# Odd layer of a two-layer transformer kernel: conversions, head norms, projection blocks and the gate term rearranged

## The chip, the cores and the metric

The kernel runs on one core of a Trainium2 chip. The metric is the device time of one execution in microseconds (us); lower is better. The time before is the median of three runs.

## What is computed

The program runs a small transformer on 256 tokens of width 1024 in fp32: an even layer (convolution and gated linear attention), a sparse expert layer, an odd layer (attention with a forget gate), a second expert layer, and a second block with two further kinds of attention and a dense network. The change touches the odd layer alone:

```python
def fox_mix(h, w_in, fgate_b, q_g, k_g, w_out):
    q, k, v, fz = jnp.split(h @ w_in, [hd, 2 * hd, 3 * hd], axis=-1)   # 16 heads of 64
    q = rms_norm(q.reshape(B, S, 16, 64), q_g)
    k = rms_norm(k.reshape(B, S, 16, 64), k_g)
    c = jnp.cumsum(jax.nn.log_sigmoid(fz + fgate_b), axis=1)
    for each half of the 256 queries:
        logits = q @ k.T * scale + c[query] - c[key], masked causally
        o = softmax(logits) @ v[:hi]
    return o @ w_out
```

## The kernel before

Everything lies with its features on the 128 partitions. The input `h` of the odd layer is held as a rounded part `hhi` and a rest `hlo` in the type fp32r; a weight is split in the same way just before it is used. A **part** is 128 x 1024 weights. ScalarE copies it to `r_sh` (`hi`, L390), VectorE subtracts to get `r_sl` (`lo`, L396), and TensorE then makes three products for each 128 rows of the contraction. There are two buffers of each kind, so `hi` of part n waits until the products of part n-2 are done (L393).

`block_T` (L419, through `mm_T`, L402) makes 24 products of 256 columns for 128 outputs; it asks for `lo` only before its last eight. `parts_R` (L429) does a quarter of the product for v, 12 products of 512 columns, and asks for `lo` at its start. Each block ends in a PSUM bank, and ScalarE evicts it (`out_ac`, `v_ac`).

The odd layer (`odd`, L1480) has 25 parts of input weights: four for q of heads 0 to 7 (NQ), one narrow one for the gate (NF), four for k (NK), four for v (NV), and the same 4, 4 and 4 for heads 8 to 15 (NQ2, NK2, NV2). Eight parts of the output weights (OUT) follow. Before the change the work runs like this:

1. The 13 parts of the first half, in a row.
2. The head norm of q and that of k: ScalarE squares 128 x 1024 numbers (to `sq` or `sqk`), TensorE sums them per head (`head_norm_pe`, L522, two products of 512 columns in fp32, which the hardware runs as four instructions), ScalarE takes logarithm (two of 512 columns) and exponential, VectorE multiplies (`head_norm_ve`, L531). One part of NQ2 stands on TensorE behind each norm.
3. A loop over 16 heads (L1662), with two further steps for the pipeline to drain. TensorE makes the logits of head i (four fp32 products: query times key for the second and the first half of the queries, and for each the gate term, whose stationary operand is a column of the identity, repeated, and whose moving operand is `fz`, the cumulated gate), then up to two **fill** items, then the transposes of head i-2 (`soft_pe_b`, L1438), then the product with v of head i-3. VectorE adds the mask and takes the row maxima (`soft_ve_a`, L1459), ScalarE the exponentials with their sums (`soft_ac_a`, L1447), VectorE scales (`soft_ve_b`, L1468), ScalarE copies the transposed probabilities (`soft_ac_b`, L1453).
4. The fill items are the ten remaining parts and, last, the two head norms of heads 8 to 15 (`fill_pe`, L1641). They are used up by heads 0 to 5.
5. ScalarE splits the eight chunks of the attention output (`ohi`), VectorE their rests (`olo`), and after all of them TensorE makes the output projection (`mm_T` over OUT), with the sums of squares for the next norm between its blocks.

Each engine runs its own list in order. What sets it is the order in which these generators are advanced: `next(fill)` stands at the same place of the loop for every engine, and on ScalarE it stands between the exponentials of head i and the copy of head i-2:

```python
                if i < 16:
                    soft_ac_a(ac, "od", i, L, sm)
                next(fill, None)
                next(fill, None)
                if 2 <= i < 18:
                    soft_ac_b(ac, "od", i - 2, PT)
```

In `fill_ac` each item is `hi` of the next part, then the eviction of this one. Weights come by DMA into a ring of four slots, two megabytes at a time; SyncE issues a load when the last `lo` that reads the slot is done.

## Time and profile before

| | |
|---|---|
| median of three runs | 2628.95 us (2627.65 to 2629.12) |
| profiled execution | 2627.96 us, its span 2626.2 us |
| TensorE (PE) busy | 2501.7 us, 95% of the span |
| VectorE (DVE), ScalarE (ACT) busy | 1690.2 us (64%), 1299.1 us (49%) |
| chain that ended last | PE 90%, ACT 4%, DVE 4% |
| mean granted clock of TensorE | 0.971 of full speed |

The span is what the hardware profiler recorded between the first and the last instruction; the execution's own time is 1.8 us more. Busy times of different engines overlap. The chain is the sequence of instructions, each waiting for the one before, that ended last. The clock of TensorE has two levels, 1.2 and 2.4 GHz; a granted clock of 0.80 in a stretch means that part of it ran at the lower one. The odd layer takes some 200 of the 2626 us, from about 1069 to 1268 us.

### The profile page before, as it was taken

Reading aid. Unit: us, or ns where it says so; the run is one execution under the profiler, and the core shown is the slowest. Engines: PE = TensorE matmul, PEld = TensorE weight load, DVE = VectorE, ACT = ScalarE, POOL = GpSimd, SP = SyncE. Lnnn points to the kernel's source line nnn. Section 1 sums busy time; section 2 is a strip of 40 time slices with the busy share of each in tenths; the row PEclk is TensorE's granted clock in tenths of the full one; section 3 lists DMA queues with packets and bytes.
Section 4 is the critical chain, followed back from the end, with each engine's and each line's share of the span. In section 5 each row is a group of like instructions: output and inputs, shape, how many; then the busy total and the mean of one; then the engine's idle time right before and its main releaser. Section 6 shows DMA issues by size and latency. Waiting matters only on the chain.

```text
span 2626.2 us, 41667 instructions
## 1 busy us (share of the span) xinstructions
PE 2501.7 (95%) x16702; PEld 2281.8 (87%) x16702; DVE 1690.2 (64%) x3116; ACT 1299.1 (49%) x2451; POOL 432.2 (16%) x389
## 2 busy tenths in 40 slices
PE   7799999999999999888999999999999997997999
PEld 7689999999988888765999999998888886877999
DVE  4734899777777777434479977775555544534654
ACT  4234444666544444434444456665444543463543
POOL 4500000388400000000000018860000000001000
PEclk9799999999999999998999999999999997999999
DMA  6103455433487777520245543346555563213342
GB/s 252 45 33 129 157 184 182 161 129 129 160 279 259 257 267 264 220 75 22 97 161 184 181 166 129 130 138 210 194 195 193 197 227 123 97 65 128 140 182 81
DMA packets 93198, 421.81 MB, mean 161 GB/s; under 512 B 10296, under 2 KB 12880, under 8 KB 85072
## 3 DMA queue, kind: packets, MB, share of 16 engines
q1 hardware_dynamic: 93008, 419.16, 46.2%
q8 instruction: 134, 2.20, 0.3%
q14 instruction: 56, 0.46, 0.1%
HBM read 415.96 MB, written 3.16 MB: 160 GB/s over the span
## 4 chain that ended last, share of the span: by engine, by line
PE 90%; ACT 4%; DVE 4%; DMA 1%; issue 1%; POOL 0%; SPq 0%; POOLq 0%; ACTq 0%; DVEq 0%
PE PS L170 89%; ACT mem L181 2%; DVE mem L191 1%; ACT r_sh L181 1%; DVE hT L199 1%; DVE r_sl L191 1%; PE PS L173 0%; DMA mem<-in_ev_in 0%; ACT r_hhi L181 0%; POOL hT L191 0%; DVE mem L205 0%; DMA mem<-in_v 0%; DMA mem<-in_ada 0%; ACT L188 0%; DVE mem L202 0%
## 5 line engine op out<-in xcount | busy, mean ns | idle before, releaser
L191 DVE TENSOR_TENSOR r_sl<-mem,r_sh 128x1024 fp32r<-128x1024 f32 (+3 forms) x742 | 890.3, 1201 | 674.8 <-ACT r_sh L181 673.9
L181 ACT ACTIVATE r_sh<-mem 128x1024 fp32r<-128x1024 f32 (+3 forms) x742 | 764.9, 1033 | 482.0 <-PE PS L170 428.0
L170 PE MATMUL PS<-r_hhi,r_sh 128*128 128x256 f32 x3280 | 839.3, 292 | 37.5 <-ACT r_hhi L181 19.8
L170 PE MATMUL PS<-r_hlo,r_sh 128*128 128x256 f32 (+1 forms) x3152 | 795.8, 289 | 5.5 <-DVE r_hlo L191 2.6
L170 PEld LDWEIGHTS PS<-r_hhi,r_sh 128*128 128x128 f32 x3280 | 641.5, 196 | 46.5 <-issue 38.9
L170 PEld LDWEIGHTS PS<-r_hlo,r_sh 128*128 128x128 f32 (+1 forms) x3152 | 614.3, 195 | 14.5 <-DVE r_hlo L191 6.5
L170 PE MATMUL PS<-r_hhi,r_sl 128*128 128x256 f32 x3280 | 469.6, 286 | 0.3 <-DVE r_sl L191 0.3
L181 ACT ACTIVATE mem<-PS 128x256 f32<-128x256 f32 (+14 forms) x633 | 217.4, 353 | 475.1 <-PE PS L170 466.0
L170 PEld LDWEIGHTS PS<-r_hhi,r_sl 128*128 128x128 f32 x3280 | 431.6, 195 | 0.8 <-DVE r_sl L191 0.5
L196 POOL TENSOR_SCALAR xT<-cst,mem 128x128 f32<-128x128 f32 x256 | 327.6, 1291 | 620.8 <-ACT mem L181 557.0
L170 PE MATMUL PS<-r_sh,r_ch 128*128 128x512 f32 x1024 | 276.5, 391 | 1.3 <-ACT r_sh L181 1.3
L170 PE MATMUL PS<-r_sl,r_ch 128*128 128x512 f32 x1024 | 274.9, 389 | 0.0
L170 PE MATMUL PS<-r_sh,r_cl 128*128 128x512 f32 x1024 | 274.8, 389 | 0.0
L170 PEld LDWEIGHTS PS<-r_sh,r_ch 128*128 128x128 f32 x1024 | 191.0, 188 | 41.7 <-ACT r_sh L181 2.6
L170 PEld LDWEIGHTS PS<-r_sl,r_ch 128*128 128x128 f32 x1024 | 192.2, 188 | 40.2
L170 PEld LDWEIGHTS PS<-r_sh,r_cl 128*128 128x128 f32 x1024 | 192.2, 188 | 40.1
L170 PE MATMUL PS<-mem 64*128 64x128 f32 (+7 forms) x1010 | 177.4, 333 | 11.8 <-DVE mem L191 8.9
L170 PEld LDWEIGHTS PS<-mem 64*128 64x128 f32 (+4 forms) x1010 | 137.0, 177 | 48.6 <-issue 19.6
L170 PE MATMUL PS<-xT 128*128 128x128 f32 x1024 | 131.5, 277 | 4.0 <-DVE xT L191 4.0
L170 PEld LDWEIGHTS PS<-xT 128*128 128x128 f32 x1024 | 124.2, 194 | 4.3 <-issue 4.3
L191 POOL TENSOR_TENSOR hT<-xT,small 128x256 f32<-128x256 f32 x12 | 10.1, 841 | 713.7 <-ACT small L181 713.7
L191 DVE TENSOR_TENSOR r_cl<-mem,r_ch 128x256 fp32r<-128x256 f32 x256 | 107.1, 418 | 2.6 <-ACT r_ch L181 2.6
(129 smaller groups left out, 2137.3 us busy)
## 6 DMA issues: line engine op xcount, KB each, us to landing
mem<-in_u SPq DMA_DIRECT2D x256, 512.0 KB, 3.3
mem<-in_v SPq DMA_DIRECT2D x256, 512.0 KB, 3.9
mem<-in_w SPq DMA_DIRECT2D x16, 2048.0 KB, 8.0
mem<-in_ada SPq DMA_DIRECT2D x48, 512.0 KB, 4.5
mem<-in_in SPq DMA_DIRECT2D x9, 2048.0 KB, 7.9
mem<-in_wq SPq DMA_DIRECT2D x8, 2048.0 KB, 7.9
mem<-in_od_in SPq DMA_DIRECT2D x6, 2048.0 KB, 10.1
mem<-in_ev_in SPq DMA_DIRECT2D x5, 2048.0 KB, 10.6
```

What stands on the lines that cost most here:

```text
L170: return self.did(self.e and self.e.matmul(out, lhsT, rhs, start=start, stop=stop, skip_group_check=skip))
L181: return self.did(self.e and self.e.activation(out, in_, func, **kw))
L191: return self.did(self.e and self.e.tensor_tensor(out, a, b, op))
L196: return self.did(self.e and self.e.tensor_scalar(out, a, s1, s2, op0, op1))
L199: return self.did(self.e and self.e.scalar_tensor_tensor(out=out, in0=a, scalar=s, in1=b, op0=op0, op1=op1))
```

## The change

- **Conversions.** `hi` of a part in the head loop now stands behind the eviction of the part two before it, and the exponentials of a head no longer stand between the end of a block and the conversion that the very next block needs. `MORE` lists the 12 parts of the second half and, new, the first two of OUT.
- **Head norms.** Those of heads 0 to 7 are taken apart and put between the first 13 parts: the sum for q behind the seventh part on TensorE, that for k behind the second part of NV. Those of heads 8 to 15 stand in `BETWEEN` as `None`, behind part 5 and behind part 7.
- **Heads.** `BETWEEN` has 14 items, two for each of heads 0 to 6; the second one now stands behind the product with v, on all engines. All 12 parts of the second half are in it.
- **Gate term.** The cumulated gate is split in a rounded part (rows 0 to 15 of `cz`) and a rest (rows 32 to 47), with the first 128 columns repeated at 256 to 384. `two` has ones in rows h and 32+h of column h. One fp32r product of 384 columns replaces the two fp32 products of a head, and it stands first, ahead of the wait for the norm of k.
- **Output.** `ohi` and `olo` of a chunk are made during the heads (`SPLIT`), and the first block of the output projection waits for one chunk at a time.

The diff, cut to its core:

```diff
-    def mm_T(pe, n, out, s, start=True, stop=True, after_norm=None):
+    def mm_T(pe, n, out, s, start=True, stop=True, after_norm=None, after=None):
...
         for k in range(a):
             if after_norm is not None:
                 pe.wait_ge("hhi", after_norm, k)
+            elif after:
+                pe.wait_ge(after[0], k)
             pe.matmul(out, h[:, k, :], s[0][:, k, :], start and k == 0, False)
             if after_norm is not None:
                 pe.wait_ge("hloP" if k % 4 == 3 else "hlo", after_norm, k)
+            elif after:
+                pe.wait_ge(after[1], k)
             pe.matmul(out, h[:, k, :], s[1][:, k, :], False, False)
         pe.wait_ge("lo", n)
         for k in range(a):
...
+        cz = in_f32r("cz", o, 384)
+        take(384)
+        two = in_f32r("two", o, 16)
...
+        MAIN = NQ + NF + NK + NV
+        MORE = NQ2 + NK2 + NV2 + OUT[0:2]
+        BANK = (0, 1, 2, 3, 4, 5, 6, 7, 2)
+
+        BETWEEN = [0, 1, 2, 3, 4, 5, None, 6, 7, None, 8, 9, 10, 11]
+
+        SPLIT = {7: 0, 8: 1, 9: 2, 10: 3, 12: 4, 14: 5, 16: 6, 18: 7}
...
+        def between_ac(ac):
+            qs, ks = qf_[:, 1024:2048], kf_[:, 1024:2048]
+            norm = 0
+            for m in BETWEEN:
+                if m is None:
+                    src, rr = (("q", 1), r) if norm == 0 else (("k", 1), rk)
+                    ln_ac(ac, rr, (6, 7), src)
+                    exp_ac(ac, rr, src)
+                    norm += 1
+                else:
+                    n = MORE[m]
+                    if m < 8:
+                        out_ac(ac, (q if m < 4 else k_)[:, 4 + m % 4, :], n, 6 + m % 2)
+                    elif m == 11:
+                        v_ac(ac, n, (6, 7), 1)
+                    hi(ac, MORE[m + 2])
+                    if m == 4:
+                        square_ac(ac, qs, sq, NQ2[3], ("q", 1))
+                    elif m == 7:
+                        square_ac(ac, ks, sqk, NK2[3], ("k", 1))
                 yield
...
+            ns = MAIN + MORE
+            hi(ac, ns[1])
+            for i, n in enumerate(MAIN):
...
-            ac.wait_ge(*ac.activation(f1[0:16, :], z16, ACT.Abs).then_inc("actC"))
-            ac.wait_ge(*ac.activation(f1[0:16, :], f1[0:16, :], ACT.Exp, scale=-1.0).then_inc("actC"))
...
-            fill = fill_ac(ac)
-            norm_q_ac(ac, 0, (0, 1, 4, 5))
-            next(fill)
-            norm_k_ac(ac, 0, (0, 1, 4, 5))
-            next(fill)
+                    v_ac(ac, n, (3, 4), 0)
+                hi(ac, ns[i + 2])
+                if i == 4:
+                    square_ac(ac, qf_[:, 0:1024], sq, NQ[3], ("q", 0))
+                elif i == 5:
+                    ac.wait_ge("out", NF[0])
+                    ac.wait_ge(*ac.activation(f1[0:16, :], z16, ACT.Abs).then_inc("actC"))
+                    ac.wait_ge(*ac.activation(f1[0:16, :], f1[0:16, :], ACT.Exp, scale=-1.0).then_inc("actC"))
+                    ac.activation(f1[0:16, :], f1[0:16, :], ACT.Ln, bias=onet[0:16, :]).then_inc("softplus", 1)
+                elif i == 6:
+                    ln_ac(ac, r, (0, 1), ("q", 0))
+                elif i == 7:
+                    exp_ac(ac, r, ("q", 0))
+                elif i == 8:
+                    square_ac(ac, kf_[:, 0:1024], sqk, NK[3], ("k", 0))
+                elif i == 10:
+                    ln_ac(ac, rk, (0, 1), ("k", 0))
+                    exp_ac(ac, rk, ("k", 0))
+            between = between_ac(ac)
             for i in range(19):
                 if i < 16:
                     soft_ac_a(ac, "od", i, L, sm)
-                next(fill, None)
-                next(fill, None)
+                next(between, None)
                 if 2 <= i < 18:
                     soft_ac_b(ac, "od", i - 2, PT)
                 if i >= 3 and (i - 3) % 2:
                     h = i - 3
                     ac.wait_ge("pv", "od", h)
                     ac.activation(oT[:, h // 2, :], PS[:, 4 + (h // 2) % 2, 0:256], COPY).then_inc("oT", h // 2)
-            for c in range(8):
-                ac.wait_ge("oT", c)
-                ac.activation(hhiv[:, c, :], oT[:, c, :], COPY).then_inc("ohi", c)
+                next(between, None)
+                if i in SPLIT:
+                    c = SPLIT[i]
+                    ac.wait_ge("oT", c)
+                    ac.wait_ge("wdone", NV2[3])
+                    ac.activation(hhiv[:, c, :], oT[:, c, :], COPY).then_inc("ohi", c)
             for c, n in enumerate(OUT):
-                hi(ac, n)
                 if c >= 2:
+                    hi(ac, n)
                     square(ac, 3, c - 2)
...
+        def between_ve(ve):
+            for m in BETWEEN:
+                if m is not None:
+                    lo(ve, MORE[m + 2])
+                if m == 7:
+                    head_norm_ve(ve, qf_[:, 1024:2048], 1024, qg, r, ("q", 1))
+                elif m == 9:
+                    head_norm_ve(ve, kf_[:, 1024:2048], 1024, P("kg", 0), rk, ("k", 1))
                 yield
...
+            for i, n in enumerate(MAIN + MORE[0:2]):
+                if i:
+                    lo(ve, n)
+                if i == 7:
+                    ve.wait_ge("softplus", 1)
+                    ve.wait_ge(*ve.scalar_tensor_tensor(f2[0:16, :], z16, 0.0, f1[0:16, :], MIN, SUB).then_inc("dveC"))
+                    ve.wait_ge(*ve.tensor_scalar(f2[0:16, :], f2[0:16, :], -1.0, MUL).then_inc("dveC"))
...
+                    ve.wait_ge(*ve.tensor_copy(cz[0:16, 0:256], z16).then_inc("dveC"))
+                    ve.wait_ge(*ve.tensor_tensor(cz[32:48, 0:256], z16, cz[0:16, 0:256].bitcast(F32), SUB).then_inc("dveC"))
+                    ve.tensor_copy(cz[0:48, 256:384], cz[0:48, 0:128].bitcast(F32)).then_inc("forget", 0)
+                elif i == 9:
+                    ve.wait_ge("qg", 0)
+                    head_norm_ve(ve, qf_[:, 0:1024], 1024, qg, r, ("q", 0))
+                elif i == 12:
+                    head_norm_ve(ve, kf_[:, 0:1024], 1024, P("kg", 0), rk, ("k", 0))
+            between = between_ve(ve)
+            for i in range(20):
                 if 2 <= i < 18:
                     soft_ve_b(ve, "od", i - 2, L, sm)
                 if i < 16:
                     soft_ve_a(ve, "od", i, L, sm, C("fmask"))
-                next(fill, None)
-                next(fill, None)
+                next(between, None)
+                next(between, None)
+                if i - 1 in SPLIT:
+                    c = SPLIT[i - 1]
+                    ve.wait_ge("ohi", c)
+                    ve.tensor_tensor(olov[:, c, :], oT[:, c, :], hhiv[:, c, :].bitcast(F32), SUB).then_inc("olo", c)
...
-                lo(ve, OUT[c])
+                if c >= 2:
+                    lo(ve, OUT[c])
...
-        def fill_pe(pe):
-            ns = NQ2 + NK2
-            for i, n in enumerate(ns):
-                block_T(pe, n, 6 + i % 2, ("out", n))
+        def between_pe(pe):
+            turn = parts_R(pe, NV2, (6, 7), ("out", NV2[3]))
+            norm = 0
+            for m in BETWEEN:
+                if m is None:
+                    head_norm_pe(pe, 1024, (sq, sqk)[norm], (6, 7), ("qk"[norm], 1))
+                    norm += 1
+                elif m < 8:
+                    block_T(pe, MORE[m], 6 + m % 2, ("out", MORE[m]))
+                else:
+                    next(turn)
                 yield
-            yield from parts_R(pe, NV2, (6, 7), ("out", NV2[3]))
-            head_norm_pe(pe, 1024, sq, (6, 7), ("q", 1))
-            yield
-            head_norm_pe(pe, 1024, sqk, (6, 7), ("k", 1))
-            yield
...
-                block_T(pe, n, i % 7, ("out", n), after_norm=None if i else 2)
-            block_R(pe, NV, (2, 3), ("out", NV[3]))
-            fill = fill_pe(pe)
-            head_norm_pe(pe, 1024, sq, (0, 1), ("q", 0))
-            next(fill)
-            head_norm_pe(pe, 1024, sqk, (4, 5), ("k", 0))
-            next(fill)
+                block_T(pe, n, BANK[i], ("out", n), after_norm=None if i else 2)
+                if i == 6:
+                    head_norm_pe(pe, 1024, sq, (0, 1), ("q", 0))
+            for u, _ in enumerate(parts_R(pe, NV, (3, 4), ("out", NV[3]))):
+                if u == 1:
+                    head_norm_pe(pe, 1024, sqk, (0, 1), ("k", 0))
+            between = between_pe(pe)
             pe.wait_ge("forget", 0)
+            pe.wait_ge("two", 0)
             for i in range(19):
                 if i < 16:
                     h, b = i, i % 2
                     rows, c = slice(64 * (h % 2), 64 * (h % 2) + 64), h // 2
                     t1, t0 = PS[:, b, 0:256], PS[:, b, 256:384]
-                    pick = ident[:, h:h + 1].broadcast_to([128, 128])
                     bank_wait(pe, b)
+                    pe.matmul(PS[:, b, 0:384], two[:, h:h + 1].broadcast_to([128, 128]), cz[:, :], True, False, skip=True)
                     pe.wait_ge("hn", ("k", h // 8))
-                    pe.matmul(t1, q[rows, c, 128:256], k_[rows, c, :], True, False, skip=True)
-                    pe.matmul(t1, pick, fz, False, True, skip=True)
-                    pe.matmul(t0, q[rows, c, 0:128], k_[rows, c, 0:128], False, False, skip=True)
-                    pe.matmul(t0, pick, fz[:, 0:128], False, True, skip=True).then_inc("logits", "od", i)
+                    pe.matmul(t1, q[rows, c, 128:256], k_[rows, c, :], False, True, skip=True)
+                    pe.matmul(t0, q[rows, c, 0:128], k_[rows, c, 0:128], False, True, skip=True).then_inc("logits", "od", i)
                     emptied[b] = ("biased", "od", i)
-                next(fill, None)
-                next(fill, None)
+                next(between, None)
                 if 2 <= i < 18:
                     soft_pe_b(pe, "od", i - 2, L, None)
                 if i >= 3:
...
                     pe.matmul(out[:, 0:256], v[:, 0, 64 * h:64 * h + 64], PT[h % 2][:, 0:256], True, False, skip=True)
                     pe.matmul(out[:, 128:256], v[:, 1, 64 * h:64 * h + 64], PT[h % 2][:, 256:384], False, True, skip=True).then_inc("pv", "od", h)
                     emptied[b] = ("oT", h // 2)
-            for c in range(8):
-                pe.wait_ge("ohi", c)
-                pe.wait_ge("olo", c)
+                next(between, None)
             for c in range(8):
                 bank_wait(pe, c)
-                mm_T(pe, OUT[c], PS[:, c, 0:256], (hhiv, olov))
+                mm_T(pe, OUT[c], PS[:, c, 0:256], (hhiv, olov), after=None if c else ("ohi", "olo"))
                 emptied[c] = ("x", 2, c)
                 if c:
                     square_sum(pe, 3, c - 1)
```

The first head, on TensorE's list. `r_sl_54` and `r_sh_51` are split weights, `mem` the queries and keys (and `fz`), `cst` the identity, `r_cz` and `r_two` the two new tiles. Before:

```order
L170 MATMUL PS<-r_hhi,r_sl_54 128x256 x7
L170 MATMUL PS<-mem 128x256 [waits s_hn,s_hn_ln,s_forget]
L170 MATMUL PS<-mem,cst 128x256
L170 MATMUL PS<-mem 128x128
L170 MATMUL PS<-mem,cst 128x128
L170 MATMUL PS<-r_hhi,r_sh_51 128x256 [waits s_hi,s_out]
```

Now:

```order
L170 MATMUL PS<-r_sh_52,r_hlo 128x512 x2
L170 MATMUL PS<-r_cz,r_two 128x384 [waits s_hn_ln,s_two,s_forget]
L170 MATMUL PS<-mem 128x256 [waits s_hn]
L170 MATMUL PS<-mem 128x128
L170 MATMUL PS<-r_hhi,r_sh_51 128x256 [waits s_hi,s_out]
```

The head now comes straight behind the last part of NV (the row of 512 columns) instead of behind the second part of NQ2, and has one product of 384 columns and two others in place of four.

ScalarE's list from the exponentials of head 1. 128x1024 rows to `r_sh` are conversions, 128x256 rows from `PS` evictions, the 128x256 and 128x128 rows from `mem` the exponentials. Before:

```order
L181 ACTIVATE mem<-mem 128x256 [waits s_rowmax]
L181 ACTIVATE mem<-mem 128x128
L181 ACTIVATE r_sh_52<-mem 128x1024
L181 ACTIVATE mem<-PS 128x256 [waits s_wdone]
L181 ACTIVATE r_sh_51<-mem 128x1024
L181 ACTIVATE mem<-PS 128x256 [waits s_wdone]
```

Now, the same place:

```order
L181 ACTIVATE mem<-mem 128x256 [waits s_rowmax]
L181 ACTIVATE mem<-mem 128x128
L181 ACTIVATE mem<-PS 128x256 [waits s_wdone]
L181 ACTIVATE r_sh_51<-mem 128x1024 [waits s_w2]
L181 ACTIVATE mem<-PS 128x256 [waits s_wdone]
L181 ACTIVATE r_sh_52<-mem 128x1024
```

The conversion moved from ahead of the eviction to behind it, and it now serves the block after the next.

ScalarE's list from the exponentials of head 4, as it is now; the row from `mem` to `mem` of 128x1024 behind `r_sh_52` is the square for the norm of k of heads 8 to 15, the next of that shape the exponential of that norm:

```order
L181 ACTIVATE mem<-mem 128x256 [waits s_rowmax]
L181 ACTIVATE mem<-mem 128x128
L181 ACTIVATE mem<-PS 128x256 [waits s_wdone]
L181 ACTIVATE r_sh_52<-mem 128x1024
L181 ACTIVATE mem<-mem 128x1024 [waits s_out]
L181 ACTIVATE mem<-PS 128x384 [waits s_pv,s_probT]
L181 ACTIVATE mem<-PS 128x256 [waits s_pv]
L181 ACTIVATE mem<-PS,small 128x512 [waits s_hn_ss,s_hn]
L181 ACTIVATE mem<-PS,small 128x512 [waits s_hn_ss]
L181 ACTIVATE mem<-mem 128x1024 [waits s_hn_ln]
```

Before, this norm stood at head 5, behind all parts; now it stands inside head 4, between an eviction and the logarithms.

## Rows read from the trace of the kernel before

**Rows 1.** Windows: stretch, length, busy PE PEld DVE ACT POOL, PEclk, DMA, GB/s
```profile
1100.90:1112.40 11.50, 11.44 (x50) 8.77 (x48) 3.67 (x3) 3.48 (x5) 0.00 (x0) 1.00 0.49 188
1112.40:1133.40 21.00, 13.02 (x57) 9.12 (x57) 6.37 (x8) 12.64 (x18) 0.00 (x0) 0.84 0.17 72
1133.40:1176.60 43.20, 39.89 (x230) 31.84 (x230) 18.39 (x33) 15.84 (x37) 0.00 (x0) 0.96 0.27 98
1176.60:1184.70 8.10, 6.23 (x28) 4.21 (x27) 1.85 (x4) 2.26 (x5) 0.00 (x0) 1.00 0.68 241
1184.70:1201.80 17.10, 10.45 (x25) 4.43 (x24) 4.43 (x9) 8.12 (x13) 0.00 (x0) 0.80 0.02 9
1201.80:1231.20 29.40, 29.40 (x139) 17.70 (x140) 16.23 (x55) 13.59 (x50) 0.00 (x0) 1.00 0.00 1
1231.20:1240.30 9.10, 4.14 (x23) 2.44 (x23) 5.10 (x18) 6.54 (x19) 0.00 (x0) 0.92 0.01 3
1240.30:1268.50 28.20, 28.19 (x205) 27.87 (x206) 12.59 (x15) 10.38 (x15) 0.00 (x0) 0.90 0.32 114
```

**Rows 2.** Timeline, PE: start, length, line, product [idle before it, what ended it]
```profile
1115.73 3.54 PE L170 MATMUL PS<-mem,cst 128*128 128x512 f32 x4 [3.39 <-ACT mem L181]
...
1128.13 1.98 PE L170 MATMUL PS<-mem,cst 128*128 128x512 f32 x4 [1.42 <-ACT mem L181]
...
1166.11 0.47 PE L170 MATMUL PS<-r_sh,r_hhi 128*128 128x512 f32 x1 [1.84 <-DVE r_sl L191]
...
1240.31 0.55 PE L170 MATMUL PS<-r_hhi,r_sh 128*128 128x256 f32 x1 [3.95 <-ACT r_sh L181]
```

**Rows 3.** Timeline, PE, a block and head 1; then two heads without fill
```profile
1138.88 0.35 PE L170 MATMUL PS<-r_hhi,r_sh 128*128 128x256 f32 x1 [0.49 <-ACT r_sh L181]
...
1141.91 0.70 PE L170 MATMUL PS<-mem 64*128 64x256 f32 x2
1142.54 0.70 PE L170 MATMUL PS<-mem,cst 128*128 128x256 f32 x2
1143.17 0.49 PE L170 MATMUL PS<-mem 64*128 64x128 f32 x2
1143.58 0.49 PE L170 MATMUL PS<-mem,cst 128*128 128x128 f32 x2
1143.83 0.36 PE L170 MATMUL PS<-r_hhi,r_sh 128*128 128x256 f32 x1
...
1208.26 0.49 PE L173 MATMUL PS<-cst,mem 128*128 128x128 f32 x3
...
1211.47 0.49 PE L173 MATMUL PS<-cst,mem 128*128 128x128 f32 x3
```

**Rows 4.** Chain of waits, head 4: mask, maxima, exponentials, conversion, rest
```profile
1173.94 0.57 DVE mem L191
...
1174.53 0.62 DVE mem L205 x2
...
1175.18 0.99 ACT mem L181 x4
1176.17 0.96 ACT r_sh L181
...
1177.14 1.24 DVE r_sl L191
```

**Rows 5.** Chain of waits, norm of k: eviction and square, second logarithm, exponential
```profile
1126.74 1.34 ACT mem L181 x2
...
1130.15 0.70 ACT mem L181
...
1130.87 1.07 ACT mem L181
```

**Rows 6.** Timeline, VectorE, scaling of one head: reciprocal, two products
```profile
1209.58 0.15 DVE L214 RECIPROCAL mem<-mem 128x2 f32<-128x2 f32 x1
1209.77 0.55 DVE L195 TENSOR_SCALAR mem<-mem 128x256 f32<-128x256 f32 x2
```

More of the change, by code:

```diff
@@ L1504, in odd @@
         fz, f1, f2 = take(256), take(256), take(256)
-        qg = take(1)
+        qg = take(8)[:, 0:1]
+        cz = in_f32r("cz", o, 384)
+        take(384)
+        two = in_f32r("two", o, 16)
+        take(16)
         assert o <= AR, o
         z16 = fz[0:16, :]
+        MAIN = NQ + NF + NK + NV
[3 more added lines that the diff above has]
+        SPLIT = {7: 0, 8: 1, 9: 2, 10: 3, 12: 4, 14: 5, 16: 6, 18: 7}
         def odd_sp(sp):
@@ L1516, in odd_po @@
             po.wait_ge("x", 1, 0)
-            po.memset(fz, 0.0).then_inc("zero", "fz")
+            po.memset(cz[:, :].bitcast(F32), 0.0).then_inc("zero", "cz")
             norm_po(po, 2, lambda c: P("od_g", c))
@@ L1537, in fill_ac, with square_ac @@
-        def fill_ac(ac):
-            ns = NQ2 + NK2 + NV2
-            hi(ac, ns[0])
-            for i, n in enumerate(ns):
-                if i + 1 < len(ns):
-                    hi(ac, ns[i + 1])
-                if i < 8:
-                    out_ac(ac, (q if i < 4 else k_)[:, 4 + i % 4, :], n, 6 + i % 2)
-                elif i == 11:
-                    v_ac(ac, n, (6, 7), 1)
+        def square_ac(ac, src, sq, last, key):
+            ac.wait_ge("out", last)
+            if key[1]:
+                ac.wait_ge("hn_ss", (key[0], 0), 512)
+            ac.activation(sq, src, ACT.Square).then_inc("hn_sq", key)
@@ new lines, in ln_ac, with exp_ac @@
+        def ln_ac(ac, r, banks, key):
+            if key[1]:
+                ac.wait_ge("hn", (key[0], 0))
+            for i in (0, 512):
+                ac.wait_ge("hn_ss", key, i)
+                ac.activation(r[:, i:i + 512], PS[:, banks[i // 512], :], ACT.Ln, scale=1.0 / 64, bias=epst).then_inc("hn_ln", key, i)
+        def exp_ac(ac, r, key):
+            ac.wait_ge("hn_ln", key, 512)
+            ac.activation(r, r, ACT.Exp, scale=-0.5).then_inc("hn_r", key)
+        def between_ac(ac):
[18 more added lines that the diff above has]
+                        square_ac(ac, ks, sqk, NK2[3], ("k", 1))
@@ L1692, in odd_pe @@
                     emptied[b] = ("oT", h // 2)
-            for c in range(8):
-                pe.wait_ge("ohi", c)
-                pe.wait_ge("olo", c)
+                next(between, None)
             for c in range(8):
                 bank_wait(pe, c)
-                mm_T(pe, OUT[c], PS[:, c, 0:256], (hhiv, olov))
+                mm_T(pe, OUT[c], PS[:, c, 0:256], (hhiv, olov), after=None if c else ("ohi", "olo"))
                 emptied[c] = ("x", 2, c)
```

48 lines of the change are left out of this document (4 added, 44 removed).

## The prediction

> **What bounds the kernel now.** I read the page first: TensorE is busy for 95% of the span and makes 90% of the chain that ended last, so time is gained only where TensorE does less, waits less, or runs at its upper clock. The windows show where that can be [rows 1]. Two kinds of stretch alternate. In the four parts of NV (1100.9 to 1112.4 us) TensorE is busy for 11.44 of 11.5 us at a clock of 1.00; nothing is to be had there. Around the norms and in the heads it isn't: idle are 8.0 us of the second window, 3.3 of the third, 1.9 of the fourth, 6.6 of the fifth and 5.0 of the seventh, 24.8 us together. The same rows give the loss to the clock: a mean of 0.84 over 21.0 us costs 0.16 x 21.0 = 3.4 us, the others 0.04 x 43.2 = 1.7, 0.20 x 17.1 = 3.4 and 0.10 x 28.2 = 2.8, together 11.3 us.
>
> The timeline says what the idle time is [rows 2]: the first norm's square (3.39 us, with 2.81 us more behind it for logarithm and exponential), the rests of late conversions (1.84 us), and the eight splits of the attention output with the conversion behind them (3.95 us). The chain shows why the conversions are late [rows 4]: mask 0.57, maxima 0.62, exponentials 0.99 us and only then the conversion, 0.96, and its rest, 1.24. A head's exponentials stand between a finished block and the weights of the next one.
>
> **The change part by part.**
>
> *Idle time, -23.8 us.* The norms of heads 0 to 7 move between the 13 parts. Each brings 1.98 us of TensorE work at full clock [rows 2], which was done before too. ScalarE has some 1.4 us of eviction and conversion in each block of 2.9 us (11.5 us by four, [rows 1]), and the steps of the norm are 1.0, 2 x 0.7 and 1.1 us [rows 5], one step a block except for k, where logarithms and exponential come to 2.5 us while TensorE has the norm and two parts, 7.8 us. The split of the gate adds three short operations of 16 partitions on VectorE between two rests; a block asks for its rest only after two thirds. I cost both at nothing; if that cover fails, what is late is a rest, at most 1.24 us for each [rows 4]. The conversion ahead of each head's second block (0.49 us) [rows 3] and those of 1.8 us go as well, since the part is now converted behind the eviction two blocks before. The 3.95 us ahead of the projection go: only the last chunk's split is left behind the last product with v, and it has fourteen products (1.7 us) to hide behind. Of the 24.8 us I leave 1.0, the drain of the last two heads, where transposes wait for scaling as before.
>
> *Clock, -11.3 us.* With those gaps the stretches at 1.2 GHz go. The first norm shows the price: 3.54 us after the gap, 1.98 us when the engine had been at work [rows 2].
>
> *Gate term, -11.8 us.* Two fp32 products go: 0.63 us (1142.54 to 1143.17) and 0.41 us (as long as the product of the same shape, 1143.17 to 1143.58) [rows 3]. The new product is not in the trace. From below: the 512-column products of NV take 11.5/48 = 0.24 us, so 384 columns take 0.18. From above: 1.04, as dear as the two that it replaces. The type is that of NV's, so I take the lower end with 0.12 for two changes between types, 0.30. That gives 16 x (1.04 - 0.30) = 11.8 us; the ends are 13.8 and 0. A head without fill falls from 3.21 us [rows 3] to 2.5.
>
> *New waits, +8.0 us.* Here I walked the four queues through the heads; time 0 is the end of a head's logits. These took 2 x (0.63 + 0.41) = 2.1 us and now take 0.63 + 0.41 + 0.30 = 1.3; transposes and the product with v take 3.21 - 2.1 = 1.1 [rows 3]. VectorE comes to head i late each time: it is held by the rest of the second block's successor, which needs eviction, conversion and rest (0.4 + 0.96 + 1.24 = 2.6 us; the eviction is 1.34 less a square of about 1.0, [rows 4, 5]) after the block's end, so until 1.3. Plain heads don't feel it: the transposes come at 2.9 and the scaling is through at 2.0 (0.7 us) [rows 6]. Three heads do.
> Head 3: its first item is a norm of 1.9 us instead of a block. ScalarE had a square to do in head 2, which puts the scaling at 2.8: 0.9 us. Then mask and maxima end at 4.0, exponentials at 5.0, the first logarithm, which frees the bank that block 6 wants, at 5.7, while TensorE is there at 3.9: 1.8 us.
> Head 4: scaling to 2.0, maxima to 3.2, exponentials to 4.2, then eviction and square (1.34) [rows 5] and a conversion between them (0.96): the square is there at 6.5. TensorE wants to sum it at 4.0. It waits 2.5 us.
> Head 7: no fill is left. Two evictions of 512 columns (1.2 us), conversion and rest of the second output part hold VectorE to 2.1, the scaling ends at 2.8, and the transposes of head 5 stand directly behind the logits: 2.8 us.
> That is 2.7 + 2.5 + 2.8 = 8.0. The ends: nothing, if the durations overlap more than rows in a chain do, and twice as much.
>
> *Clock behind the new waits, +3.4 us.* The gap of 1.84 us was followed by 1.7 us of loss (third window), that of 1.87 us by none (fourth window: 8.1 - 6.23 us idle, clock 1.00) [rows 1, 2]. So I count 1.7 us for two of three. [...]
>
> *DMA.* No load is added. The loads of the ring follow the last rest that reads a slot, and all rests come earlier; the DMA engines are at most 0.68 busy in these windows [rows 1]. Cost nothing; the last four loads, those of the next layer's queries, move with the parts that free their slots.
>
> Sum: -23.8 - 11.3 - 11.8 + 8.0 + 3.4 = **-35.5 us**. All of it lies on TensorE's own queue, which the chain follows, and what comes after the odd layer starts that much earlier. The profiled execution took 2627.96 us, so 2592.5; it was 1.0 us under the median of 2628.95, so I forecast **2593.5 us**.
>
> **The rivals.**
>
> *A, the new waits are hidden.* If the squares and rests come in time, the 8.0 and 3.4 us stay in hand: 2582 us. For it: ScalarE is busy for only 15.8 of 43.2 us in the third window. Against it: its queue is in order, and the square has to stand behind the exponentials. 0.13.
>
> *B, the softmax chain binds the heads without fill.* TensorE asks for 2.5 us a head; VectorE has 1.2 + 0.7 + 0.4 = 2.3 us (mask and maxima, scaling, one rest of the output), ScalarE as much with the split. If the period stays near 3.2 us, eight heads give back 8 x 0.7 = 5.6 us: 2599; with the waits doubled as well, 2607. For it: nothing is left between the three. Against it: the sixth window has VectorE idle for 13 of 29 us while TensorE never waits. 0.13.
>
> *C, slower: the clock stays down.* The waits of heads 3, 4 and 7, and heads in which TensorE has short breaks, could put it at 1.2 GHz from head 7 to the end of the projection. That is 8 x 2.5 + (28.2 - 2.8) = 45 us of work, which would take 45 us more: 2638.5 us. It decides the sign from 35 us on. For it: clocks of 0.80 and 0.84 in windows with gaps. Against it: the eighth window starts behind a gap of 3.95 us and loses only 2.8 us, so the clock returns under dense products. 0.03.
>
> *D, the change does not do what it says.* If the norms merely wait elsewhere, since each needs an evicted block, gate term, projection gap and its clock remain: 11.8 + 3.95 + 2.8 = 18.6 us, 2610.5 us. Against it: the walk through the first 13 parts left no wait. 0.03.
>
> **How the numbers follow.** The forecast, -30 to -41 us, has 0.66, A and B 0.13 each, C and D 0.03, and 0.02 is left for no change. A change of 0.2%, 5.3 us, is about what a measurement of this kernel can tell. Faster: 0.66 + 0.13 + 0.13 + 0.03 = 0.95; same 0.02; slower 0.03. The range goes from A's 2582 to 2606, just short of B's far end.
>
> **What would show it.** In the profile after: no idle time over 0.5 us between 1069 us and the first logits; those come at about 1116; r_cz products of 0.2 to 0.3 us; idle of 1 to 3 us ahead of block 6, ahead of the sum of squares for k in head 4 and ahead of the transposes in head 7; 2.5 us from head to head after that; the projection directly behind the last product with v, at about 1204; PEclk at 0.95 or more throughout. I am wrong if the heads without fill stay above 3 us, if a wait for a DMA appears, or if the second stretch of the heads runs at a clock under 0.9.

## The result, and the profile after

| | before | after |
|---|---|---|
| median | 2628.3 us (2627.17 to 2629.12, four runs) | 2606.2 us (2603.51 to 2607.58, four runs) |
| ratio | | 0.9916, 95% interval 0.9901 to 0.9931 |
| profiled execution | 2627.96 us | 2607.58 us |
| mean granted clock of TensorE | 0.971 | 0.967 |

The change makes the kernel faster, by 22.1 us between the medians and by 20.4 us between the two profiled executions. I had forecast 35.5 us and a range that ends at 2606.0 us, so the time lies just outside it. The clock says where to look: the changed kernel waits less and yet runs at a lower mean clock. Page of the changed kernel, busy times and the granted clock in 40 slices:

```profile
PE 2497.5 (96%) x16654; PEld 2281.0 (88%) x16654; DVE 1691.0 (65%) x3120; ACT 1298.0 (50%) x2451; POOL 432.2 (17%) x389
PEclk9799999999999999996999999999999997999999
```

The slice of about 65 us that holds the heads without fill has fallen to 6 tenths. Windows of the changed kernel, with the columns of [rows 1], from the first logits to behind the middle of the projection:

```profile
1115.98:1148.18 32.20, 29.92 (x203) 26.51 (x202) 14.14 (x25) 17.40 (x37) 0.00 (x0) 0.95 0.41 157
1148.18:1157.67 9.49, 7.07 (x42) 5.19 (x41) 5.55 (x11) 5.59 (x12) 0.00 (x0) 0.97 0.01 2
1157.67:1164.00 6.33, 6.33 (x15) 4.25 (x14) 1.59 (x5) 2.94 (x7) 0.00 (x0) 0.50 0.00 0
1164.00:1178.70 14.70, 14.42 (x65) 10.44 (x63) 6.57 (x10) 5.96 (x12) 0.00 (x0) 1.00 0.39 143
1178.70:1181.80 3.10, 0.09 (x1) 0.00 (x0) 1.90 (x5) 1.13 (x2) 0.00 (x0) 0.87 0.00 0
1181.80:1222.20 40.40, 40.40 (x110) 24.12 (x110) 18.69 (x63) 15.96 (x56) 0.00 (x0) 0.50 0.00 1
1222.20:1224.40 2.20, 2.17 (x13) 1.24 (x11) 0.42 (x1) 1.18 (x3) 0.00 (x0) 1.00 0.00 0
1224.40:1250.80 26.40, 26.26 (x207) 25.52 (x206) 11.30 (x16) 10.45 (x17) 0.00 (x0) 1.00 0.37 131
```

Read the third number (busy TensorE) against the second, and then the clock. From the first logits on, idle time is left in four places only, 8.2 us together; before it was 24.8 us [rows 1]. But for 40.4 us TensorE is busy without a break at 0.50 of its clock, that is at 1.2 GHz. The same heads ran at 1.00 before (the sixth window of [rows 1]). The timeline of TensorE in the changed kernel names the waits, and the period of the heads behind them:

```profile
1115.98 0.34 PE L170 MATMUL PS<-r_cz,r_two 128*128 128x384 f32 x1
1116.25 0.92 PE L170 MATMUL PS<-mem 64*128 64x256 f32 x4
...
1141.22 0.55 PE L173 MATMUL PS<-cst,mem 128*128 128x128 f32 x3 [0.93 <-DVE mem L195]
...
1143.92 0.58 PE L170 MATMUL PS<-r_hhi,r_sh 128*128 128x256 f32 x1 [1.35 <-ACT mem L181]
...
1155.97 2.69 PE L170 MATMUL PS<-mem,cst 128*128 128x512 f32 x4 [2.42 <-ACT mem L181]
...
1177.61 0.34 PE L170 MATMUL PS<-r_cz,r_two 128*128 128x384 f32 x1
1181.81 0.90 PE L173 MATMUL PS<-cst,mem 128*128 128x128 f32 x3 [3.02 <-DVE mem L195]
...
1186.30 0.90 PE L173 MATMUL PS<-cst,mem 128*128 128x128 f32 x3
...
1217.79 0.91 PE L173 MATMUL PS<-cst,mem 128*128 128x128 f32 x3
...
1222.25 0.55 PE L173 MATMUL PS<-cst,mem 128*128 128x128 f32 x3
...
1224.41 0.39 PE L170 MATMUL PS<-r_hhi,r_sh 128*128 128x256 f32 x1
```

The heads without fill come every 4.49 us (1181.81 to 1186.30), and the projection starts at 1224.41. The last logits end at 1217.79; behind them stand only transposes and products with v, and there the clock comes back, at about 1222.0, before the first block of the projection. VectorE in the changed kernel, ahead of the wait of 3.02 us:

```profile
1179.87 1.23 DVE L191 TENSOR_TENSOR r_sl<-mem,r_sh 128x1024 fp32r<-128x1024 f32 x1 [2.13 <-ACT r_sh L181]
1181.01 0.15 DVE L214 RECIPROCAL mem<-mem 128x2 f32<-128x2 f32 x1
1181.20 0.55 DVE L195 TENSOR_SCALAR mem<-mem 128x256 f32<-128x256 f32 x2
```

The scaling that the transposes wait for (L195) stands behind the rest of the second output part, a weight that is used more than 40 us later, and that rest waits for ScalarE.

### The profile page after: what moved, and what is told of

Same layout as the page of the kernel before. It is cut to its first block, busy times and chain, and to the rows that moved or that the text cites. A ratio compares the mean times of both kernels' runs of the same rounds, so it can differ in the third digit from the quotient of the medians.

```text
span 2605.8 us, 41569 instructions
## 1 busy us (share of the span) xinstructions
PE 2497.5 (96%) x16654; PEld 2281.0 (88%) x16654; DVE 1691.0 (65%) x3120; ACT 1298.0 (50%) x2451; POOL 432.2 (17%) x389
## 4 chain that ended last, share of the span: by engine, by line
PE 91%; DVE 4%; ACT 3%; issue 1%; DMA 1%; POOL 0%; SPq 0%; POOLq 0%; ACTq 0%; DVEq 0%
PE PS L170 90%; ACT mem L181 1%; DVE mem L191 1%; ACT r_sh L181 1%; PE PS L173 1%; DVE r_sl L191 1%; DVE hT L199 1%; DMA mem<-in_ev_in 0%; POOL hT L191 0%; DMA mem<-in_v 0%; ACT r_hhi L181 0%; ACT L188 0%; DVE mem L202 0%; DVE mem L205 0%; ACT xT L181 0%
## 5 line engine op out<-in xcount | busy, mean ns | idle before, releaser
L170 PE MATMUL PS<-mem 64*128 64x128 f32 (+7 forms) x1010 | 187.1, 347 | 11.2 <-DVE mem L191 8.9
L170 PEld LDWEIGHTS PS<-mem 64*128 64x128 f32 (+4 forms) x1010 | 145.5, 185 | 51.4 <-issue 22.7
L181 ACT ACTIVATE mem<-mem 128x128 f32<-128x128 f32 (+9 forms) x117 | 62.3, 543 | 99.8 <-DVE mem L205 83.6
```

The lines of the kernel that those rows point to most:

```text
L170: return self.did(self.e and self.e.matmul(out, lhsT, rhs, start=start, stop=stop, skip_group_check=skip))
L181: return self.did(self.e and self.e.activation(out, in_, func, **kw))
```

## Experiments

In the diffs, lines without a sign are there to find the place. Each run was compared with the kernel before on the same chip. The medians of the kernel before differ by up to 1.9 us between the chips, and so far a difference between two runs of this list is uncertain. "The change" is the changed kernel (median 2606.2 us).

### e1: the rest of the second output part two heads later

```diff
             for m in BETWEEN:
-                if m is not None:
+                if m is not None and m < 11:
                     lo(ve, MORE[m + 2])
...
                 next(between, None)
+                if i == 8:
+                    lo(ve, MORE[13])
```

> The change with one difference: VectorE makes the rest of the second output part in head 8 instead of in front of head 7, so nothing holds the scaling that the transposes of head 7 wait for (3.02 us in the profile after). Theory 1 (that wait puts TensorE at 1.2 GHz, and the work of the later heads can't bring it back, but would keep it up): no wait, a clock of 1.00 in heads 7 to 15, 2.4 us from head to head instead of 4.5, and the projection about 3 + 20 us earlier, so about 2583 us. Theory 2 (the work of these heads can't hold the clock either): only the wait goes, heads 7 to 15 still run at a clock near 0.50, about 2603 us.

Measured: 2588.96 us (2582.79 to 2590.96), ratio 0.9847 (0.983 to 0.9865). TensorE of e1 in the heads without fill, and one window of them:

```profile
1183.62 0.55 PE L173 MATMUL PS<-cst,mem 128*128 128x128 f32 x3 [0.93 <-DVE mem L195]
...
1184.89 0.44 PE L170 MATMUL PS<-r_cz,r_two 128*128 128x384 f32 x1
1185.26 0.92 PE L170 MATMUL PS<-mem 64*128 64x256 f32 x4
...
1187.38 0.44 PE L170 MATMUL PS<-r_cz,r_two 128*128 128x384 f32 x1
```

```profile
1190.00:1200.00 10.00, 9.92 (x48) 6.40 (x48) 7.86 (x27) 6.84 (x25) 0.00 (x0) 1.00 0.00 1
```

One VectorE operation of 1.23 us, moved from the end of step 6 of the loop to the end of step 8, gives 17.2 us. The wait of 3.02 us is gone; one of 0.93 us stands two heads later, behind the moved rest. The clock stays at 1.00, heads come every 2.49 us (1184.89 to 1187.38), and the projection starts at 1204.37. The forecast of theory 1, 2583 us, took the whole wait as gone and was 6 us too low, theory 2 was 14 us too high; the clock decides for theory 1. And the softmax chain does not bind these heads: rival B falls.

### e2: the gate term again as two fp32 products

```diff
-                    pe.matmul(PS[:, b, 0:384], two[:, h:h + 1].broadcast_to([128, 128]), cz[:, :], True, False, skip=True)
                     pe.wait_ge("hn", ("k", h // 8))
...
+                    pe.matmul(t1, pick, fz, False, True, skip=True)
...
+                    pe.matmul(t0, pick, fz[:, 0:128], False, True, skip=True).then_inc("logits", "od", i)
```

> The change with the gate term again as two fp32 products a head. Theory 1 and 2 (which products a head holds decides whether the clock comes back): the clock is back at 1.00 a few microseconds into the heads without fill, 3.2 us from head to head instead of 4.5, nine times 1.3 us gained, against 0.77 us lost in each of seven heads with fill: about 2600 us, faster than the change although TensorE has more to do. Theory 3 (the clock is held down by the wait or by chance, whatever the products are): the heads take 2 x 3.2 = 6.4 us each and the time is about 2628 us.

Measured: 2614.07 us (2605.1 to 2619.0, six runs), ratio 0.9942 (0.9925 to 0.9959), between the two forecasts. The profiled execution was the slowest of the six. Windows of e2, and TensorE at head 7 and behind it:

```profile
1200.00:1210.00 10.00, 10.00 (x25) 5.34 (x25) 3.78 (x14) 3.41 (x12) 0.00 (x0) 0.50 0.00 0
```

```profile
1181.89 0.66 PE L173 MATMUL PS<-cst,mem 128*128 128x128 f32 x3 [1.95 <-DVE mem L195]
...
1187.56 0.85 PE L173 MATMUL PS<-cst,mem 128*128 128x128 f32 x3
...
1193.42 0.85 PE L173 MATMUL PS<-cst,mem 128*128 128x128 f32 x3
```

A wait of 1.95 us was enough here, and the heads then ran at 0.50, every 5.86 us, up to the projection. The heads of the kernel before had just these products and held 1.00. So the kind of the gate product is not what keeps the clock down in the heads; the same products ran at either level, and what differs is the level at which they were entered. My thought that the fp32 gate products would bring it back fell.

### e3: four more products in each head without fill

```diff
                     emptied[b] = ("biased", "od", i)
+                    if 7 <= i < 16:
+                        bank_wait(pe, 7)
+                        for _ in range(4):
+                            pe.matmul(PS[:, 7, 0:384], two[:, h:h + 1].broadcast_to([128, 128]), cz[:, :], True, True, skip=True)
```

> The change with four more fp32r products of 384 columns in each of heads 7 to 15, into a bank that is free; their result is not read. Theory 1 and 2: the denser work brings the clock back, about 2.4 + 0.7 = 3.1 us a head instead of 4.5: nine times 1.4 us less, about 2594 us. Theory 3 (no kind of work in these heads brings it back): four times 0.34 us more in each of nine heads at the lower clock, about 2618 us.

Measured: 2602.11 us (2599.06 to 2603.43), ratio 0.99 (0.9884 to 0.9917). Windows of e3:

```profile
1181.00:1190.00 9.00, 9.00 (x24) 5.86 (x24) 3.06 (x12) 3.82 (x13) 0.00 (x0) 0.50 0.01 2
1190.00:1199.00 9.00, 9.00 (x27) 6.38 (x26) 4.26 (x14) 2.91 (x11) 0.00 (x0) 0.50 0.00 0
1199.00:1212.00 13.00, 13.00 (x63) 9.24 (x63) 6.83 (x22) 5.89 (x20) 0.00 (x0) 0.96 0.00 0
```

The added products of head 7 also stand ahead of the wait, which is 1.90 us here (up to 1180.26). The clock comes back with a little more work per head, but only at about 1200.0, almost 20 us behind the wait, and the 36 added products cost time of their own. Most of the forecast gain (2594) did not come. That the added work brought it back, and not chance, is argued from one trace and from the mean clocks: 0.970 to 0.973 in the four runs of e3, 0.967 or 0.968 in those of the change.

### e4: the kernel before with the new gate term alone

```diff
-                    pe.matmul(t1, pick, fz, False, True, skip=True)
...
-                    pe.matmul(t0, pick, fz[:, 0:128], False, True, skip=True).then_inc("logits", "od", i)
+                    pe.matmul(PS[:, b, 0:384], two[:, h:h + 1].broadcast_to([128, 128]), cz[:, :], True, False, skip=True)
```

> The kernel before with nothing but the gate term as one fp32r product. Theory 1 and 2: behind the norms of heads 8 to 15, whose waits put the clock down before as well (0.80), it now does not come back, so ten heads take 4.5 us instead of 3.2: 13 us lost against some 3 us gained in heads 0 to 5, about 2638 us, slower than the kernel before although 30 products are gone. As forecast (the product is only cheaper): ten heads at 2.4 us and less in the others, about 2616 us.

Measured: 2610.37 us (2609.6 to 2615.47), ratio 0.9941 (0.9924 to 0.9958). Windows and TensorE of e4, where the norms of heads 8 to 15 stand behind all parts:

```profile
1180.00:1190.00 10.00, 7.19 (x11) 2.50 (x11) 1.28 (x1) 4.95 (x7) 0.00 (x0) 0.50 0.00 0
...
1200.00:1210.00 10.00, 10.00 (x50) 6.54 (x50) 7.17 (x24) 6.04 (x24) 0.00 (x0) 1.00 0.01 2
```

```profile
1179.22 3.22 PE L170 MATMUL PS<-mem,cst 128*128 128x512 f32 x4 [3.26 <-ACT mem L181]
...
1185.26 3.78 PE L170 MATMUL PS<-mem,cst 128*128 128x512 f32 x4 [2.81 <-ACT mem L181]
```

Two waits of about 3 us lower the clock here too, but the sums of squares, eight fp32 instructions over the whole array, come behind them. The clock is back at 1190.0, 1.2 us behind the second sum, and it stays. From this came the theory that the next two runs try: in heads without fill the clock stays where it is, up or down (theory P), and denser products raise it. Measured so, the gate term alone is worth 17.4 us between the medians, 11 to 20 us by the interval, so my 11.8 is at its lower end. In a head with two blocks the period falls from 8.54 us (1138.88 [rows 3] to 1147.42) to 7.49 (1144.09 to 1151.58 in e4). Of these 1.05 us, 0.2 are a shorter wait for the conversion (0.49 to 0.29), and 0.85 are work, where I had 0.74. Part of the gain is clock: before, the gap of 1.84 us [rows 2] was followed by a clock of 0.64 over 3.9 us; the gap of 1.68 us that stands there in e4 was followed by 1.00.

### e5: one burst behind the wait

```diff
                     emptied[b] = ("oT", h // 2)
+                if i == 7:
+                    bank_wait(pe, 7)
+                    for _ in range(16):
+                        pe.matmul(PS[:, 7, 0:384], two[:, 0:1].broadcast_to([128, 128]), cz[:, :], True, True, skip=True)
```

> The change with sixteen more fp32r products of 384 columns, once, behind the product with v in head 7, that is right behind the wait of 3 us; their result is not read. Theory P (in the heads without fill the clock stays where it is, up or down, and only work that fills the whole array, as projection blocks and the sums of the norms do, brings it back): the products run at the lower clock at first (0.34 us each), the clock comes back within about 6 us, and heads 8 to 15 take 2.5 us each: 2606 - 8 x 2.0 + 5 = about 2595 us. Theory R (the clock comes back when it will, whatever runs): 5 us more, about 2611 us.

Measured: 2592.97 us (2590.27 to 2595.1), ratio 0.9865 (0.9849 to 0.9882). TensorE of e5 from the wait on, and windows of the burst and the heads:

```profile
1181.19 0.90 PE L173 MATMUL PS<-cst,mem 128*128 128x128 f32 x3 [3.02 <-DVE mem L195]
1182.02 1.54 PE L170 MATMUL PS<-mem 128*64 128x256 f32 x4
1183.49 4.95 PE L170 MATMUL PS<-r_cz,r_two 128*128 128x384 f32 x17
...
1190.50 0.44 PE L170 MATMUL PS<-r_cz,r_two 128*128 128x384 f32 x1
```

```profile
1183.49:1188.38 4.89, 4.89 (x19) 4.64 (x18) 0.00 (x0) 0.45 (x2) 0.00 (x0) 0.61 0.01 3
1188.38:1209.00 20.62, 19.64 (x96) 12.86 (x95) 16.34 (x54) 13.45 (x49) 0.00 (x0) 1.00 0.00 0
```

The wait of 3.02 us is untouched, work is added whose result nobody reads, and the kernel is 13.2 us faster than the change. The clock came back within the burst and stayed for the remaining heads. Theory P stands, and theory R (2611) falls: all four runs are below 2595.2.

### e6: e1 with a wait put back later

```diff
             for i in range(20):
+                if i == 10:
+                    for _ in range(5):
+                        ve.wait_ge(*ve.tensor_scalar(rk, rk, 1.0, MUL).then_inc("dveC"))
                 if 2 <= i < 18:
```

> The kernel with the late rest (2589 us) with VectorE made to do five products of 128 x 1024 on a tile that nobody needs, once, ahead of the scaling in head 10, so that TensorE waits there some 3 to 5 us, with the clock up until then. Theory P: behind that wait the clock is at 0.50 to the end of the heads, six heads of 2.0 us more on top of the wait: about 2589 + 4 + 12 = 2605 us. Theory R, or that the products alone decide (they held the clock at 1.00 before): only the wait and one short dip, 2589 + 4 + 2 = about 2595 us.

Measured: 2599.36 us (2595.96 to 2603.7), ratio 0.9899 (0.9882 to 0.9915), between the two forecasts. The profiled execution was the fastest of the four. Windows of e6, and TensorE at the delayed head:

```profile
1158.00:1164.00 6.00, 6.00 (x28) 4.42 (x27) 1.22 (x1) 2.63 (x7) 0.00 (x0) 1.00 0.00 0
...
1184.85:1210.00 25.15, 25.15 (x69) 15.06 (x70) 12.20 (x42) 10.24 (x36) 0.00 (x0) 0.50 0.00 0
```

```profile
1184.85 0.90 PE L173 MATMUL PS<-cst,mem 128*128 128x128 f32 x3 [3.19 <-DVE mem L195]
...
1189.35 0.90 PE L173 MATMUL PS<-cst,mem 128*128 128x128 f32 x3
```

The time alone would not decide; the windows do. One wait of 3.19 us was followed by 25 us at 0.50 and heads of 4.50 us. The difference to 2605 is in the profiled execution a gain elsewhere: behind the wait of 2.41 us in head 4, and behind those of 0.92 and 1.36 in head 3, all within 0.01 us as long as in e1, the clock stayed at 1.00 this time; in e1 the low clock there costs 5.1 us.

### e7: the norms of heads 8 to 15 an item later

```diff
-        BETWEEN = [0, 1, 2, 3, 4, 5, None, 6, 7, None, 8, 9, 10, 11]
+        BETWEEN = [0, 1, 2, 3, 4, 5, 6, None, 7, -1, None, 8, 9, 10, 11]
```

An item of -1 is empty; the late rest of e1 is kept, one step further back.

> The kernel with the late rest, and the norms of heads 8 to 15 one item later: the norm of q behind part 6, that of k at the start of head 5 instead of the end of head 4. If the waits of 0.93, 1.35 and 2.42 us in heads 3 and 4 are due to squares and banks that come too late, as the walk through the queues said, they shrink to under 1 us together, and the 6 us at a clock of 0.5 behind the last of them go as well: 2589 - 4 - 3 = about 2582 us. If the norms wait wherever they are put, about 2589 us.

Measured: 2584.25 us (2581.78 to 2588.7), ratio 0.9838 (0.9822 to 0.9855). Of the waits for ScalarE in heads 3 and 4 two are left, 1.12 us for the square of q and 1.45 us for a bank, and with them a clock of 0.75 between 1158 and 1164 us. So the waits shrank from 4.7 to 2.6 us together, not to under 1 as expected, and the low clock is shorter but not gone.

### e8: e1 with the output split behind the last head, as before

```diff
-                if i in SPLIT:
-                    c = SPLIT[i]
-                    ac.wait_ge("oT", c)
-                    ac.wait_ge("wdone", NV2[3])
-                    ac.activation(hhiv[:, c, :], oT[:, c, :], COPY).then_inc("ohi", c)
+            for c in range(8):
+                ac.wait_ge("oT", c)
+                ac.activation(hhiv[:, c, :], oT[:, c, :], COPY).then_inc("ohi", c)
```

VectorE's rests move likewise.

> The kernel with the late rest, with the attention output again split for all eight chunks behind the last head. The conversion of the first output parts is early in both. If the split during the heads is worth the wait ahead of the projection and the clock behind it, as forecast less the conversion of 0.95 us: 2.7 us of wait and up to 2.8 us of clock come back, 2592 to 2595 us. If the split was as good as hidden, or costs as much in the heads, 2589 us.

Measured: 2589.11 us (2588.8 to 2590.08), ratio 0.9855 (0.9838 to 0.9871). TensorE of e8 at the start of the projection:

```profile
1205.98 0.36 PE L170 MATMUL PS<-r_hhi,r_sh 128*128 128x256 f32 x1 [0.87 <-ACT r_hhi L181]
```

Against e1's 2588.96 that is no difference. What filled the 3.95 us ahead of the projection was mostly the conversion behind the splits and TensorE's wait for all eight chunks; with an early conversion and a wait for each chunk, 0.87 us are left. No run tells the two apart.

### e9: e1 with the gate term as two fp32 products

The diffs of e1 and e2 together.

> The kernel with the late rest (2589 us), the clock up in its last heads, with the gate term again as two fp32 products a head. This sizes the gate term by itself. As forecast, 1.04 us for two fp32 products against 0.30 (0.27 to 0.38 in the profile after), in sixteen heads: about 11 us more, 2600 us. If the clock should fall in the heads with this mix, as the profile of the change with the gate term put back (2614 us) leaves possible, 2615 us or more.

Measured: 2594.99 us (2593.93 to 2595.27), ratio 0.987 (0.9854 to 0.9887). TensorE of e9 in the heads without fill:

```profile
1187.20 0.55 PE L173 MATMUL PS<-cst,mem 128*128 128x128 f32 x3 [0.22 <-DVE mem L195]
...
1190.46 0.49 PE L173 MATMUL PS<-cst,mem 128*128 128x128 f32 x3
...
1193.67 0.49 PE L173 MATMUL PS<-cst,mem 128*128 128x128 f32 x3
```

With the clock up in the last heads, the gate term is worth 6.0 us between the medians of e9 and e1 (3 to 12 us between their runs), not the 11 that were expected. The heads without fill do fall from 3.21 to 2.49 us, nine times 0.72. But e1 gives part back: slower heads hide waits (0.22 us in e9 where e1 has 0.93; 1.54 in head 4 where e1 has 2.42; 1.11 in head 3 where e1 has 2.28), and behind those of heads 3 and 4 e1 has low clocks worth 5.1 us while e9 shows 1.00 throughout.

### e10: a version that beats both

```diff
-        BETWEEN = [0, 1, 2, 3, 4, 5, 6, None, 7, -1, None, 8, 9, 10, 11]
+        BETWEEN = [0, 1, 2, 3, 4, 5, 6, None, 7, -1, None, -1, 8, 9, 10, 11]
...
-                    ln_ac(ac, rr, (6, 7), src)
+                    ln_ac(ac, rr, (6, 7) if norm else (7, 6), src)
```

It starts from e7 (the first line is e7's), gives the second norm an empty item behind it, and swaps the two banks of the first.

> The kernel with the later norms (2584 us), with two more differences: the norm of q puts its first sum in the bank that is free already, and nothing stands in head 5 behind the norm of k, so that its logarithms have left the banks before the next part of v wants one; the parts of v move on to heads 6 and 7. If the waits of 1.12 and 1.45 us left there are those of these banks, they go, with the low clock behind the second (a mean of 0.75 over 6 us): 2584 - 2.6 - 1.5 = about 2580 us. If they are only moved, 2584 us.

Measured: 2580.35 us (2579.91 to 2581.91), ratio 0.9815 (0.9799 to 0.9832). Windows of e10:

```profile
1150.00:1158.00 8.00, 7.79 (x37) 4.73 (x35) 4.75 (x11) 5.02 (x14) 0.00 (x0) 1.00 0.00 0
1158.00:1164.00 6.00, 5.76 (x28) 4.39 (x27) 2.40 (x4) 4.80 (x11) 0.00 (x0) 1.00 0.00 0
```

The waits for ScalarE are down to one of 0.24 us, those for VectorE's scaling to four, the longest 1.02 us. The clock is 1.00 from the first logits to the projection, which starts at 1199.15. It is 25.9 us faster than the change with the same operations, dealt out otherwise. The four runs span 2.0 us, where those of the change span 4.1 and those of e2 13.9. That fits a clock that falls or returns at other points from run to run. The traces show one execution each; of the others there is the mean clock, and in e2 it goes with the time: 0.972 in the fastest run, 0.965 to 0.967 in the three slowest.

## Why the prediction was wrong, point by point

| step | forecast | measured in the changed kernel |
|---|---|---|
| first logits | about 1116 | 1115.98 |
| head 3, scaling and bank | 0.9 and 1.8 | 0.93 and 1.35 |
| head 4, square for k | 2.5 | 2.42 |
| head 7, scaling behind a rest | 2.8 | 3.02 |
| gate product, start to next start | 0.30 | 0.27 behind a block; 0.37 in heads without fill (e1) |
| heads without fill at full clock | 2.5 | 2.49 (e1) |
| clock behind the new waits | 3.4 | 1.7 + 3.4 + 17.8 |
| projection | about 1204, directly behind v | 1224.41, directly behind v |

**Idle time, -23.8, and new waits, +8.0: right.** The four gaps of the windows are those that the walk through the queues found, and a wait of 0.28 us; together they are 8.0 us. No DMA wait appeared.

**Gate term, -11.8: right in its price; its worth depends on the rest.** By the rows it is 7 x (1.04 - 0.27) + 9 x (1.04 - 0.37) = 11.4 us. Taken alone it gave 17.4 us (e4) and on top of e1 6.0 (e9), since it also changes waits and, with them, the clock.

**Clock, -11.3: right for what was there before.** From 1100 to 1140 us and in the projection TensorE runs at 1.00.

**Clock behind the new waits, +3.4: this step failed.** I took 1.7 us for two of three waits, from the gap of 1.84 us in the third window of [rows 1]. Behind the waits of head 3 that is what came: windows of the changed kernel,

```profile
1140.00:1144.00 4.00, 1.72 (x9) 0.86 (x8) 2.20 (x7) 1.69 (x6) 0.00 (x0) 0.93 0.62 193
1144.00:1148.00 4.00, 4.00 (x23) 4.00 (x24) 0.00 (x0) 1.87 (x3) 0.00 (x0) 0.64 0.78 332
```

so 4 x 0.07 + 4 x 0.36 = 1.7 us. Behind the wait of head 4 it was 9.49 x 0.03 + 6.33 x 0.50 = 3.4. Behind that of head 7 eight heads took 4.49 instead of 2.49 us, 16.0, and the drain behind the last logits 1.8 more than in e1: 17.8 us. The starts of the projection say the same: 1224.41 less e1's 1204.37 are 20.0, less 1.2 by which the layer starts later and 1.1 of longer waits, 17.8 again. Both gaps on which I built the price (1.84 and 1.87 us) were followed by blocks of weights; the one of head 7 has neither a block nor a norm's sum behind it. In my rows the clock had come back under that work, and I booked the price to the gap as if any work would do; e1, e5 and e6 show that in these heads it does not.

With 22.9 in place of 3.4 the sum would be 2612.0 us for the profiled execution; it took 2607.58. Of the 4.4 us between, 1.6 lie outside the odd layer: it starts 0.5 us later than before (1070.11 for 1069.58), and from the product ahead of the next layer's wait (1269.44 before, 1251.19 now) to the end of the span the changed kernel needs 2.1 us less, 1.7 of them because the low clock behind that wait, 2.6 us in both, ends sooner. e1 shows nothing of that second gain, so I take it for luck and not for a part of the change. Idle time is 0.8 us less than I left, and the gate term with what filled heads gain in e4 is 12.0 instead of 11.8. The remaining 1.8 us I leave open.

**The rivals.** A was wrong, the waits came. B fell with e1. D fell: idle time went from 24.8 to 8.2 us. C had the mechanism, in heads 8 to 15 alone: the clock was back at 1222.0, and the projection ran at 1.00. I gave it 0.03 because the projection of before recovered behind a gap of 3.95 us, and did not ask whether heads without fill would recover as blocks do. Its price of 2.5 us more for each head was too high, 2.0 was measured. C with that end would have been 18 us over the forecast, and the range should have reached to about 2612. The text named the sign, a second stretch of heads at a clock under 0.9, and that is what the profile shows.

## What to carry to other kernels

Price a new wait on TensorE by the work that follows it, not by its length: here waits of 2.3 to 3 us cost nothing to 3.4 us of clock ahead of weight blocks and norm sums, and 18 us ahead of light work that never idles. Ahead of such a stretch, look at each operation that the other engines have in front of what TensorE waits for, and move what is not due yet; one rest of 1.23 us was worth 17 us. Where the wait can't be moved, heavy work right behind it can pay even if nobody reads its result (e5). When a kernel gains less than its idle time did, compare the granted clock by windows before looking for new waits.

## What the runs showed of the hardware

- Being busy did not bring the clock back. TensorE was busy for 40.4 of 40.4 us at 0.50 in the changed kernel, 50 us long in e2, and 25 us in e6, in heads that hold logits over 64 rows, a gate product, transposes of 128 columns and products with v over 64 columns of the array. The same heads at 1.00 stayed there (29.4 us before [rows 1], 20.6 in e5). The Trainium skill, page "TensorE: Matmul & The Clock Gate", Part 1, says that activity releases the throttle; the runs agree for weight blocks, norm sums and the burst of e5 (17 products of 384 columns, 4.9 us at a mean of 0.61), and not for these heads.
- With the same transposes and products with v, but no logits between them, the clock came back: in the changed kernel 4.2 us behind the last logits (1217.79 to 1222.0), in e2 4.8 us (1228.58 to 1233.4), in e6 3.0 us (1207.34 to 1210.4), each time before the first block of the projection. So what stayed at 0.50 is the mix with the logits and the gate product. Why, no run shows.
- A wait's length decides only in part. Between the first norm and the projection every wait of 3.0 us or more was followed by 0.50. That of 2.41 to 2.43 us in head 4 was in the change, e1, e3, e5 and e8, and in e6 it was not. Waits of 1.95 us (e2), 1.90 (e3) and 1.84 (before) were; 1.87 (before) [rows 1], 1.68 and 1.66 (e4) and 1.54 (e2, e9) were not, but 1.45 in e7 was. The pair of 0.93 and 1.35 us in head 3 was in the change, e1, e3, e5 and e8, and in e6 it was not.
- A product in fp32r of 384 columns took 0.27 us from start to start behind a block of its own type, and 0.37 between fp32 products; the two fp32 products that it replaces took 1.04 [rows 3].
